# mLSTM by whole chunks of eight heads: queries scaled beforehand, one sum per head, weights of the late query/key units split ahead

## The chip, the cores and the metric

One core of a Trainium2 chip. The metric is the device time of one execution in microseconds. Before the change three executions took 1109.45, 1111.19 and 1111.83 us.

## The reference, cut to what matters

Two decoder layers on 512 tokens of width 1024. Layer 0 mixes tokens with an mLSTM (eight heads, query/key width 64, value width 128), layer 1 with sliding-window attention; each is followed by a gated MLP with a short convolution, and each half has RMSNorm before and behind it. The change lies in the mLSTM. Per head and chunk, with q already times 1/8:

```python
b = jnp.cumsum(lfb, axis=-1)
inter = b + m[..., None]
dlog = b[..., :, None] - b[..., None, :] + igb[..., None, :]
dlog = jnp.where(causal, dlog, -jnp.inf)
m_t = jnp.maximum(inter, jnp.max(dlog, axis=-1))
w = jnp.einsum('bhtd,bhsd->bhts', qb, kb) * jnp.exp(dlog - m_t[..., None])
s_inter = jnp.exp(inter - m_t)
num = jnp.einsum('bhts,bhsv->bhtv', w, vb) + s_inter[..., None] * jnp.einsum('bhtd,bhdv->bhtv', qb, C)
den = jnp.sum(w, axis=-1) + s_inter * jnp.einsum('bhtd,bhd->bht', qb, n)
hout = num / jnp.maximum(jnp.abs(den), jnp.exp(-m_t))[..., None]
C_new = decay[..., None, None] * C + jnp.einsum('bhs,bhsd,bhsv->bhdv', ws, kb, vb)
```

The output is then normalised per head, multiplied by sigmoid(o), where o is another projection of the input, and projected by `m_w_out`.

## The kernel before, in words

**Splitting.** Every large product runs as three fast matmuls on operands in two parts: ScalarE rounds a raw weight tile to the high part (`split_hi`, L535), VectorE subtracts it from the raw tile for the low part (`split_lo`, L884), TensorE multiplies hi by hi, hi by lo, lo by hi (L1435 to L1437 in `project`). Weights come as units of 128 x 1024 (512 KB) in a fixed order: four query/key units loaded at once (`first_units`), a gate unit, query/key units 4 to 7, eight value units, eight units of o, eight of `m_w_out`. SP loads a raw unit as soon as the one four places before it in its slot has been split.

**Order.** There is no planner. Each engine has one queue written out by hand in its block (`sync`, `gpsimd`, `scalar`, `vector`, `tensor`), and semaphores join them. An engine works strictly in the order of its block.

**Query/key units.** ScalarE splits units 4 and 5, then takes the row statistics, then the gate chain on 8 x 512 rows (two tanh, an exponential, a logarithm, with table loads), and after that units 6 and 7. VectorE splits 4 and 5, waits for the gate sums, copies units 0 to 3 out of PSUM (`copy_qk`, L965), does the scans of the gates, and then in one loop (L990) splits unit n + 2 and copies unit n.

**mLSTM steps.** Chunks are of 128 tokens (four). The code takes half of the heads at a time: eight steps `s`, chunk `s // 2`, four heads each (`four(s)`). In step `s` TensorE projects unit `s` of o into bank 6 or 7, then in `combine(s)` multiplies queries by the old state C (L1575, banks 3 and 4), keys by values for the new state (L1580), and weights by values for the numerators (L1584, banks 2 and 5); then `keys(s + 1)` (L1560) makes the next scores. VectorE in `outputs` scales the old-state product by exp(inter - m) (L1086), adds the numerators (L1089) and takes the denominators (L1095, L1096), in `state` decays and adds C (L1069, L1070), in `weigh` multiplies scores by exponentials (L1055), in `weights` makes the exponents of the next step (L1046) and in `scale_o` scales unit `s` of o (L1039). ScalarE takes the exponential (L651), splits a weight unit, takes the tanh of o (L667) and the squares of a finished step (`squares`, L628). GpSimd scales o by the head norm (L504) and broadcasts a chunk's rows u to all partitions through DRAM (L490).

**End of the stage.** The last unit of o is projected in two halves of 256 tokens, with the last `combine` and the transposes of chunk 0 (`turn_heads`, L1598) between them. `out_block(c, ...)` (L1629 to L1631) then multiplies chunk c by the eight units of `m_w_out`; in block 0 each unit k is first needed as TensorE comes to it. `scale_heads`, `gate_heads` and `gated_lo` on VectorE and `gated_hi` on ScalarE prepare chunk c.

## Time and profile before

| | |
|---|---|
| median of three runs | 1111.19 us |
| profiled execution | 1110.87 us, its span 1108.6 us |
| TensorE matmul busy | 1095.0 us (99%) |
| VectorE, ScalarE, GpSimd busy | 539.3, 430.7, 45.5 us |
| mean granted TensorE clock | 0.997 |

The span runs from the first to the last instruction; all positions in microseconds count from its start. TensorE is the engine that is almost always busy; the others have idle time of which most costs nothing. What can be gained or lost in a stage is read from what TensorE waits for there and how far apart its matmuls start.

### The profile page before, as it was taken

To read this page: it belongs to the slowest core of one execution; us is meant where nothing else is said; L and a number is where in the kernel's file an instruction comes from. 1 tells how busy PE (TensorE), PEld (TensorE's weight loads), DVE (VectorE), ACT (ScalarE), POOL (GpSimd) and SP (SyncE) were. 2 spreads that over 40 slices of the span, in tenths; PEclk is the share of its full clock that TensorE was granted. 3 is DMA by queue.
4 is the path that set the end of the run, shared out by engine and by line. 5 is a ranking of instruction groups with operands and counts; after the bars stand their busy time and mean duration, and the time that the engine had idled before them with its cause. 6 is when DMAs were issued, how large, how long until landed. Compare 5 with 4: busy or idle time off the path is not lost.

```text
span 1108.6 us, 14797 instructions
## 1 busy us (share of the span) xinstructions
PE 1095.0 (99%) x5562; PEld 912.9 (82%) x5562; DVE 539.3 (49%) x820; ACT 430.7 (39%) x753; POOL 45.5 (4%) x45
## 2 busy tenths in 40 slices
PE   9999999999999999999999999999999999999997
PEld 7788777898888888888889987789888888888886
DVE  6534678654344444333356486664444444423344
ACT  6511356443323232322255277754232323422242
POOL 1000110000000000000002023200000000000000
PEclk9999999999999999999999999999999999999999
DMA  9332226024333323122362542023323232303231
GB/s 283 121 97 77 82 96 203 3 82 124 95 102 88 112 77 114 38 79 99 105 182 67 147 102 77 1 58 95 105 84 113 77 114 77 112 28 103 96 132 77
DMA packets 141509, 108.72 MB, mean 98 GB/s; under 512 B 22424, under 2 KB 127000, under 8 KB 141472
## 3 DMA queue, kind: packets, MB, share of 16 engines
q1 hardware_dynamic: 140576, 105.83, 32.2%
q0 software_dynamic: 608, 2.11, 0.6%
q8 instruction: 25, 0.41, 0.1%
q10 hardware_dynamic: 288, 0.27, 0.1%
q14 instruction: 12, 0.10, 0.0%
HBM read 106.08 MB, written 2.11 MB: 98 GB/s over the span
## 4 chain that ended last, share of the span: by engine, by line
PE 92%; DVE 4%; ACT 3%; issue 1%; POOL 0%; DVEq 0%; ACTq 0%; POOLq 0%
PE ps L1435 17%; PE ps L1437 17%; PE ps L1436 17%; PE ps L1686 7%; PE ps L1685 7%; PE ps L1684 7%; PE ps L1629 3%; PE ps L1631 2%; PE ps L1630 2%; PE ps L1519 1%; PE ps L1521 1%; PE ps L1520 1%; PE ps L1774 1%; PE ps L1803 1%; PE ps L1785 1%; DVE w_lo L884 1%
## 5 line engine op out<-in xcount | busy, mean ns | idle before, releaser
L1435 PE MATMUL ps<-act_hi,w_hi 128*128 128x512 f32 (+1 forms) x1016 | 369.2, 363 | 2.8 <-DVE w_lo L884 2.6
L1436 PE MATMUL ps<-act_lo,w_hi 128*128 128x512 f32 (+1 forms) x1016 | 367.0, 361 | 0.0
L1437 PE MATMUL ps<-act_hi,w_lo 128*128 128x512 f32 (+1 forms) x1016 | 366.9, 361 | 0.0
L1435 PEld LDWEIGHTS ps<-act_hi,w_hi 128*128 128x128 f32 x1016 | 192.1, 189 | 33.8 <-DVE w_lo L884 3.1
L1437 PEld LDWEIGHTS ps<-act_hi,w_lo 128*128 128x128 f32 x1016 | 192.1, 189 | 29.5
L1436 PEld LDWEIGHTS ps<-act_lo,w_hi 128*128 128x128 f32 x1016 | 192.2, 189 | 29.0
L1684 PE MATMUL ps<-w_hi 128*128 128x512 f32 x288 | 112.0, 389 | 0.0
L1685 PE MATMUL ps<-w_lo,w_hi 128*128 128x512 f32 x288 | 112.0, 389 | 0.0
L1686 PE MATMUL ps<-w_hi,w_lo 128*128 128x512 f32 x288 | 112.0, 389 | 0.0
L717 ACT ACTIVATE arena<-ps,vecs 128x512 f32<-128x512 f32 x44 | 34.3, 779 | 188.6 <-PE ps L1437 188.6
L1216 DVE SCALAR_TENSOR_TENSOR arena<-ps,vecs,arena 128x511 f32<-128x511 f32 x44 | 33.0, 749 | 144.5 <-ACT arena L717 144.4
L711 ACT CAST w_hi<-raw 128x1024 fp32r<-128x1024 f32 x80 | 83.1, 1044 | 39.4 <-PE ps L1437 39.4
L1250 DVE TENSOR_TENSOR w_lo<-raw,w_hi 128x1024 fp32r<-128x1024 f32 x32 | 39.2, 1225 | 119.9 <-ACT w_hi L742 119.9
L1208 DVE TENSOR_TENSOR w_lo<-raw,w_hi 128x1024 fp32r<-128x1024 f32 x80 | 94.0, 1217 | 0.2
L535 ACT CAST w_hi<-raw 128x1024 fp32r<-128x1024 f32 x66 | 68.0, 1046 | 64.5 <-PE ps L1437 26.9
L1225 DVE TENSOR_TENSOR arena<-ps,arena 128x512 f32 (+1 forms) x44 | 30.4, 692 | 117.2 <-PE ps L1437 113.5
L742 ACT CAST w_hi<-raw 128x1024 fp32r<-128x1024 f32 x32 | 33.8, 1055 | 129.1 <-PE ps L1686 129.1
L884 DVE TENSOR_TENSOR w_lo<-raw,w_hi 128x1024 fp32r<-128x1024 f32 x64 | 77.0, 1217 | 7.0 <-ACT w_hi L535 7.0
L1685 PEld LDWEIGHTS ps<-w_lo,w_hi 128*128 128x128 f32 x288 | 54.1, 188 | 11.3
L1684 PEld LDWEIGHTS ps<-w_hi 128*128 128x128 f32 x288 | 54.1, 188 | 11.2
L1686 PEld LDWEIGHTS ps<-w_hi,w_lo 128*128 128x128 f32 x288 | 54.1, 188 | 11.1
L721 ACT ACTIVATE arena<-arena 128x512 f32<-128x512 f32 x44 | 27.8, 632 | 79.6 <-DVE arena L1220 79.6
(209 smaller groups left out, 1226.1 us busy)
## 6 DMA issues: line engine op xcount, KB each, us to landing
raw<-in_f_w_up SPq DMA_DIRECT2D x88, 512.0 KB, 4.6
raw<-in_f_w_down SPq DMA_DIRECT2D x44, 512.0 KB, 3.3
raw<-in_m_w_in SPq DMA_DIRECT2D x23, 512.0 KB, 4.6
raw<-in_m_w_out SPq DMA_DIRECT2D x8, 512.0 KB, 3.5
raw<-in_a_w_in SPq DMA_DIRECT2D x16, 256.0 KB, 4.3
raw<-in_a_w_out SPq DMA_DIRECT2D x16, 256.0 KB, 4.7
h<-in_x SPq DMA_DIRECT2D x4, 512.0 KB, 7.2
h<-in_x_turned SPq DMA_DIRECT2D x3, 512.0 KB, 8.0
```

The source lines that it names most:

```text
L535: nc.scalar.copy(w_hi[:, s], raw[:, s % 4]).then_inc(w_hi_done, 1)
L711: nc.scalar.copy(w_hi[:, 4 + s], raw[:, s]).then_inc(w_hi_done, 1)
L717: nc.scalar.activation(cv[:, t], ps[:, 2 * t], ACT.Identity, scale=taps[l][:, 2, bass.ds(f, 1)], bias=taps[l][:, 3, bass.ds(f, 1)]).then_i ...
L884: nc.vector.tensor_tensor(w_lo[:, s], raw[:, s % 4], w_hi[:, s].bitcast(F32), ALU.subtract).then_inc(w_lo_done, 1)
L1208: nc.vector.tensor_tensor(w_lo[:, 4 + s], raw[:, s], w_hi[:, 4 + s].bitcast(F32), ALU.subtract).then_inc(w_lo_done, 1)
L1250: nc.vector.tensor_tensor(w_lo[:, j], raw[:, j], w_hi[:, j].bitcast(F32), ALU.subtract).then_inc(w_lo_done, 1)
L1435: nc.tensor.matmul(dst, uh[:, k], zh, start=(k == 0), stop=False)
L1436: nc.tensor.matmul(dst, uh[:, k], zl, start=False, stop=False)
L1437: ins = nc.tensor.matmul(dst, ul[:, k], zh, start=False, stop=(k == KT - 1))
L1684: nc.tensor.matmul(dst, hi[:, bs], w_hi[:, s, hs], start=start, stop=False)
L1685: nc.tensor.matmul(dst, hi[:, bs], w_lo[:, s, hs], start=False, stop=False)
L1686: return nc.tensor.matmul(dst, lo[:, bs], w_hi[:, s, hs], start=False, stop=stop)
```

## The change

- **Chunks.** `combine`, `keys`, `weigh`, `state`, `outputs`, `weights` and the exponential take a chunk of eight heads at once: four times instead of eight. TensorE projects two units of o in a row, then runs old state, next scores, new state and numerators of the chunk.
- **One sum.** The old-state product and the numerators go into the same place in PSUM (banks 2 to 5) and are added there. For that the queries of chunks 1 to 3 are multiplied by exp(inter - m) before the product, on GpSimd, after the unscaled ones have made their scores. The factors come to all partitions by three more transfers through DRAM (`s_dram`, `s_all`). The factor 1/8 moves into `copy_qk`. VectorE's L1086 and L1089 become two plain copies a chunk.
- **Units split ahead.** ScalarE and VectorE split query/key units 4 to 7 all together, ahead of the gate chain.
- **Last unit of o in halves.** `scale_o`, tanh and the head-norm scale of the last unit run per half. The squares of the last chunk's first half come behind the cast of output unit 4.
- **Places and queues.** C and the factors lie in `h`, so the rows of x for blocks 1 to 3 are loaded at the end of the stage instead of early; `g_col` is loaded by SP, ahead of x, instead of by ScalarE's queue.

```diff
-        ew = arena[:, E:E + 4 * KB].rearrange("p (b t q) -> p b t q", b=2, t=HG)
+        ew = arena[:, E:E + 8 * KB].rearrange("p (b h q) -> p b h q", b=2, h=MH)
         I = E + 4 * KB
-        itmp = arena[:, I:I + HG * DV1].rearrange("p (t q) -> p t q", t=HG)
-        C = arena[:, I + HG * DV1:I + 2 * HG * DV1].rearrange("p (t q) -> p t q", t=HG)
+        h_flat = h[:].rearrange("p b f -> p (b f)")
+        s_all = h_flat[:, D:D + HG * 3 * P].rearrange("p (t q) -> p t q", t=HG)
+        C = h_flat[:, D + HG * 3 * P:D + HG * 3 * P + HG * DV1].rearrange("p (t q) -> p t q", t=HG)
...
+        PAIRS = [(t, g, 2 * t + g) for t in range(HG) for g in range(2)]
+        def out_at(t, g):
+            return 2 + 2 * (t // 2) + g, slice(t % 2 * DV1, (t % 2 + 1) * DV1)
...
+            nc.sync.dma_start(g_col[:], columns[:, 0:KT]).then_inc(g_col_in, 16)
...
             sp.wait_ge(sum_done, KT - 1)
-            for b in range(NB - 1):
-                nc.sync.dma_start(h[:, b], x[0, b * P:(b + 1) * P]).then_inc(x_in[b], 16)
+            nc.sync.dma_start(h[:, 0], x[0, 0:P]).then_inc(x_in[0], 16)
...
-            sp.wait_ge(e_raw, NS)
+            sp.wait_ge(e_raw, NB)
             gains(norm_mix_post[0], norm_ffn_pre[0])
-            sp.wait_ge(os_done, O_UNITS)
-            nc.sync.dma_start(h[:, NB - 1], x[0, (NB - 1) * P:]).then_inc(x_in[NB - 1], 16)
+            sp.wait_ge(os_done, O_UNITS + 1)
+            for b in range(1, NB):
+                nc.sync.dma_start(h[:, b], x[0, b * P:(b + 1) * P]).then_inc(x_in[b], 16)
...
+            pool.wait_ge(row_act, 2)
+            nc.gpsimd.dma_start(s_dram.ap(), rows[:, 6]).then_inc(s_out, 16)
+            pool.wait_ge(s_out, 16)
+            for g in range(2):
+                nc.gpsimd.dma_start(s_all[g * DK:(g + 1) * DK], s_dram.ap()
+                                    .rearrange("(t g) q -> g t q", g=2)[g][:, P:].partition_broadcast(DK))\
+                    .then_inc(s_in, 16)
+            pool.wait_ge(s_in, 32)
             for n in range(O_UNITS):
                 if n in (2, 4):
-                    pool.wait_ge(e_raw, n)
+                    pool.wait_ge(e_raw, n // 2)
                     u_everywhere(n // 2 + 1)
+                for half in range(2 if n == O_UNITS - 1 else 1):
+                    ts = slice(half * S // 2, (half + 1) * S // 2) if n == O_UNITS - 1 else slice(0, S)
+                    pool.wait_ge(o_tanh, n + half + 1)
+                    nc.gpsimd.tensor_scalar(o_sig[:, n, ts], o_sig[:, n, ts], hn_half[:, n:n + 1],
+                                            hn_half[:, n:n + 1], ALU.mult, ALU.add).then_inc(o_done, 1)
+                if n in (1, 3, 5):
+                    c = n // 2 + 1
+                    pool.wait_ge(st_mm, c + 1)
+                    q_c = qk_t[:, 0:HG, c * P:(c + 1) * P]
+                    nc.gpsimd.tensor_tensor(q_c, q_c, s_all[:, :, (c - 1) * P:c * P], ALU.mult)\
+                        .then_inc(qs_done, 1)
...
-            split_hi(g_qk(4))
-            split_hi(g_qk(5))
+            for n in range(FIRST, QK_UNITS):
+                split_hi(g_qk(n))
...
-            for n in range(6, QK_UNITS):
-                split_hi(g_qk(n))
...
+            exponents(0)
+            for c in range(NB):
+                split_hi(G_O + 2 * c + 1)
+                if c >= 1:
+                    squares(2 * c - 2)
+                tanh_o(2 * c, 2 * c + 1)
+                if c < NB - 1:
+                    exponents(c + 1)
+                    split_hi(G_O + 2 * c + 2)
+                else:
                     for k in range(2):
                         split_hi(G_MOUT + k)
...
+                if c >= 1:
+                    squares(2 * c - 1)
+                if c < NB - 1:
+                    tanh_o(2 * c + 1, 2 * c + 2)
+                if c == NB - 2:
                     nc.scalar.preload_act_table_set(LN_EXP_SET)
                     rms_heads(1, slice(0, 2 * MH))
                     nc.scalar.preload_act_table_set(EXP_TANH_SET)
...
+            tanh_o(NS - 1, NS, 0, S // 2)
+            for k in range(2, 4):
+                split_hi(G_MOUT + k)
+            gated_hi(0, 0)
+            tanh_o(NS - 1, NS + 1, S // 2, S)
             nc.scalar.preload_act_table_set(LN_EXP_SET)
             split_hi(G_MOUT + 4)
             gated_hi(0, 1)
+            squares(NS - 2)
             squares(NS - 1)
             split_hi(G_MOUT + 5)
...
-            split_lo(g_qk(4))
-            split_lo(g_qk(5))
+            for n in range(FIRST, QK_UNITS):
+                split_lo(g_qk(n))
...
-                nc.vector.tensor_tensor(qk_t[:, n], ps[:, qk_bank(n)], rs_row, ALU.mult).then_inc(pj_used, 1)
+                if n < HG:
+                    ins = nc.vector.scalar_tensor_tensor(qk_t[:, n], ps[:, qk_bank(n)], DK ** -0.5, rs_row,
+                                                         ALU.mult, ALU.mult)
+                else:
+                    ins = nc.vector.tensor_tensor(qk_t[:, n], ps[:, qk_bank(n)], rs_row, ALU.mult)
+                ins.then_inc(pj_used, 1)
...
             for n in range(FIRST, QK_UNITS):
-                split_lo(g_qk(n + 2) if n + 2 < QK_UNITS else G_V + n + 2 - QK_UNITS)
                 copy_qk(n)
+                if n >= QK_UNITS - 2:
+                    split_lo(G_V + n - (QK_UNITS - 2))
...
+            def weigh(c):
+                dve.wait_ge(e_exp, c + 1)
+                dve.wait_ge(st_mm, c + 1)
+                e = ew[:, c % 2].rearrange("p (g t) q -> p g (t q)", g=2)
+                nc.vector.tensor_tensor(e, ps[:, 0:2], e, ALU.mult).then_inc(w_done, 1)
+            def state(c):
                 if c == NB - 1:
                     return
+                dve.wait_ge(n_mm, c + 1)
+                new = ps[:, 2:2 + HG, STATE]
                 if c == 0:
+                    ins = nc.vector.tensor_copy(C, new)
                 else:
+                    dec = decay_own[:, :, c].unsqueeze(2).to_broadcast([P, HG, DV1])
+                    link(nc.vector.tensor_tensor(C, C, dec, ALU.mult))
+                    ins = nc.vector.tensor_tensor(C, C, new, ALU.add)
                 ins.then_inc(c_done, 1)
...
+            def outputs(c):
+                dve.wait_ge(n_mm, c + 1)
+                for a in range(2):
+                    ins = nc.vector.tensor_copy(
+                        v_tok[:, c, 4 * a:4 * a + 4].rearrange("p (b g) v -> p g b v", g=2),
+                        ps[:, 2 + 2 * a:4 + 2 * a, 0:2 * DV1].rearrange("p g (b v) -> p g b v", v=DV1))
                 ins.then_inc(num_done, 1)
+                dve.wait_ge(num_done, c + 1)
+                den = v_tok[:, c, :, DV]
                 link(nc.vector.scalar_tensor_tensor(dtmp[:], den, -1.0, den, ALU.mult, ALU.max))
+                link(nc.vector.tensor_tensor(dm[:, c], dtmp[:], gt[:, c, 3], ALU.max))
...
             weights(0)
...
+            for c in range(NB):
+                if c >= 1:
+                    outputs(c - 1)
+                    state(c - 1)
+                weigh(c)
+                split_lo(G_O + 2 * c + 1)
+                if c < NB - 1:
+                    weights(c + 1)
+                else:
+                    finish_factors(1, 0, 2)
+                    scale_heads(0)
+                scale_o(2 * c, (w_used, counted(G_O + 2 * c)))
+                if c < NB - 1:
+                    split_lo(G_O + 2 * c + 2)
+                    scale_o(2 * c + 1, (w_used, counted(G_O + 2 * c + 1)))
+                if c == NB - 2:
                     head_factors(0, 2)
-                if s < NS - 1:
-                    scale_o(s)
-            finish_factors(1, 0, 2)
-            scale_heads(0)
+            split_lo(G_MOUT)
+            scale_o(NS - 1, (oh_mm, 1), 0, S // 2)
+            split_lo(G_MOUT + 1)
             split_lo(G_MOUT + 2)
-            outputs(NS - 1)
+            outputs(NB - 1)
             gate_heads(0, 0)
             scale_heads(1)
             gated_lo(0, 0)
-            scale_o(NS - 1)
+            gate_heads(0, 1)
+            scale_o(NS - 1, (w_used, counted(G_O + NS - 1)), S // 2, S)
             split_lo(G_MOUT + 3)
-            gate_heads(0, 1)
             split_lo(G_MOUT + 4)
             gated_lo(0, 1)
             head_factors(2, NB)
...
+            def keys(c):
+                cs = slice(c * P, (c + 1) * P)
+                if c >= 1:
+                    pe.wait_ge(w_done, c)
+                for t, g, hd in PAIRS:
                     pr = slice(g * DK, (g + 1) * DK)
+                    ins = nc.tensor.matmul(ps[:, g, t * P:(t + 1) * P], qk_t[pr, HG + t, cs], qk_t[pr, t, cs],
+                                           start=True, stop=True)
                 ins.then_inc(st_mm, 1)
+            def combine(c):
                 cs = slice(c * P, (c + 1) * P)
                 if c > 0:
+                    pe.wait_ge(num_done, c)
+                    pe.wait_ge(c_done, c)
+                    pe.wait_ge(qs_done, c)
+                    for t, g, hd in PAIRS:
                         pr = slice(g * DK, (g + 1) * DK)
+                        bank, cols = out_at(t, g)
+                        nc.tensor.matmul(ps[:, bank, cols], qk_t[pr, t, cs], C[pr, t], start=(t % 2 == 0),
+                                         stop=False)
                 if c < NB - 1:
+                    keys(c + 1)
+                    for t, g, hd in PAIRS:
                         pr = slice(g * DK, (g + 1) * DK)
...
+                        nc.tensor.matmul(ps[pr, 2 + t, STATE], kw[:, c, hd * DK:(hd + 1) * DK],
+                                         v_tok[:, c, hd], start=(c == 0), stop=False)
+                pe.wait_ge(w_done, c + 1)
+                for t, g, hd in PAIRS:
+                    bank, cols = out_at(t, g)
+                    ins = nc.tensor.matmul(ps[:, bank, cols], ew[:, c % 2, HG * g + t], v_tok[:, c, hd],
+                                           start=False, stop=(t % 2 == 1))
                 ins.then_inc(n_mm, 1)
...
                 if s < NS - 1:
                     project(SLOT[g], 6 + s % 2).then_inc(w_used, 1)
-                    combine(s)
-                    keys(s + 1)
+                    if s % 2:
+                        combine(s // 2)
                 else:
-                    project(SLOT[g], 6 + s % 2, 0, S // 2)
-                    combine(s)
+                    project(SLOT[g], 6 + s % 2, 0, S // 2).then_inc(oh_mm, 1)
+                    combine(NB - 1)
                     turn_heads(0)
+                    pe.wait_ge(os_done, NS)
                     project(SLOT[g], 6 + s % 2, S // 2, S).then_inc(w_used, 1)
...
```

## Rows read from the trace of the kernel before

**Rows 1.** The page, part 1: busy us (share) and instructions of each engine.

```profile
PE 1095.0 (99%) x5562; PEld 912.9 (82%) x5562; DVE 539.3 (49%) x820; ACT 430.7 (39%) x753; POOL 45.5 (4%) x45
```

**Rows 2.** Windows: length, busy us (instructions) PE, PEld, DVE, ACT, POOL; clock, DMA, GB/s.

```profile
46.70:49.90 3.20, 3.13 (x8) 2.51 (x9) 2.61 (x5) 3.20 (x9) 0.92 (x2) 0.53 0.61 172
...
106.28:188.68 82.40, 80.62 (x506) 64.86 (x505) 62.42 (x123) 40.10 (x106) 7.40 (x10) 1.00 0.39 122
...
175.00:189.00 14.00, 12.84 (x57) 9.85 (x58) 12.33 (x18) 9.45 (x20) 1.01 (x1) 1.00 0.82 243
```

**Rows 3.** TensorE's waits: line, releaser: us in total, times, longest us.

```profile
PE ps L1435 <- DVE w_lo L884: 2.6, 1, 2.6
...
PE ps L1629 <- DVE w_lo L884: 1.1, 2, 0.9
...
PE ps L1598 <- DVE arena L1117: 0.4, 1, 0.4
```

**Rows 4.** Timeline, TensorE, 43 to 50: start, us, instruction, [idle before <- releaser].

```profile
43.75 0.39 PE L1437 MATMUL ps<-act_hi,w_lo 128*128 128x512 f32 x1
46.77 0.79 PE L1435 MATMUL ps<-act_hi,w_hi 128*128 128x512 f32 x1 [2.63 <-DVE w_lo L884]
...
49.85 0.39 PE L1436 MATMUL ps<-act_lo,w_hi 128*128 128x512 f32 x1
```

**Rows 5.** Timeline, VectorE: the low half of unit 6.

```profile
45.51 1.21 DVE L884 TENSOR_TENSOR w_lo<-raw,w_hi 128x1024 fp32r<-128x1024 f32 x1
```

**Rows 6.** Timeline, TensorE, one mLSTM step; the second L1580 row is cut at 129.65.

```profile
128.89 0.72 PE L1575 MATMUL ps<-arena 64*128 64x129 f32 x8
129.54 0.66 PE L1580 MATMUL ps<-arena 128*64 128x129 f32 x8
...
129.70 0.50 PE L1580 MATMUL ps<-arena 128*64 128x129 f32 x6
...
130.13 1.16 PE L1584 MATMUL ps<-arena 128*128 128x129 f32 x8
131.22 0.71 PE L1560 MATMUL ps<-arena 64*128 64x128 f32 x8
131.86 0.50 PE L1435 MATMUL ps<-act_hi,w_hi 128*128 128x512 f32 x1
```

**Rows 7.** Groups of ScalarE, 20 to 240: shapes, count | busy, mean ns | idle before.

```profile
L535 ACT CAST w_hi<-raw 128x1024 fp32r<-128x1024 f32 x32 | 32.6, 1043 | 33.7 <-PE ps L1521 25.0 <-PE ps L1437 7.8 <-DMA raw<-in_m_w_in 0.8
L628 ACT ACTIVATE junk<-arena 128x128 bf16<-128x128 f32 x32 | 9.4, 294 | 0.0
```

**Rows 8.** Timeline, VectorE, behind the numerators of one step.

```profile
148.65 0.70 DVE L1086 TENSOR_TENSOR arena<-ps,gt 128x516 f32<-128x516 f32 x1 [1.64 <-PE ps L1584]
...
150.11 0.17 DVE L1095 SCALAR_TENSOR_TENSOR dtmp<-arena 128x4 f32<-128x4 f32 x1
...
150.51 0.43 DVE L1069 TENSOR_TENSOR arena<-arena,decay_own 128x258 f32<-128x258 f32 x1
...
151.31 0.68 DVE L1055 SCALAR_TENSOR_TENSOR arena<-ps,arena 128x512 f32<-128x512 f32 x1
151.91 1.13 DVE L1046 SCALAR_TENSOR_TENSOR arena<-g_pre,gt,causal 128x128 f32<-128x128 f32 x4
```

**Rows 9.** Groups of VectorE, 20 to 240: one that reads 1024 columns of PSUM.

```profile
L917 DVE TENSOR_TENSOR act_lo<-ps,act_hi 128x1024 fp32r<-128x1024 f32 x4 | 4.9, 1222 | 6.8 <-ACT act_hi L568 6.8
```

**Rows 10.** Groups of GpSimd over the span.

```profile
L504 POOL TENSOR_SCALAR arena<-arena,hn_half 128x512 f32<-128x512 f32 x8 | 6.4, 796 | 120.0 <-ACT arena L667 120.0
...
L516 POOL TENSOR_TENSOR arena<-arena,asm 128x512 f32<-128x512 f32 x4 | 4.2, 1040 | 50.1 <-DVE asm L1357 50.1
```

**Rows 11.** The line of u's broadcasts, L490: from issue to landing.

```profile
DMA to landing us min/median/max: 3.9/5.2/7.6
```

**Rows 12.** Timeline, GpSimd: the last hn scale, beside a split on VectorE.

```profile
176.86 1.01 POOL L504 TENSOR_SCALAR arena<-arena,hn_half 128x512 f32<-128x512 f32 x1 [9.64 <-ACT arena L667]
```

**Rows 13.** Timeline, TensorE: the first matmul of output block 0.

```profile
175.80 0.48 PE L1629 MATMUL ps<-w_hi,act_hi 128*128 128x512 f32 x1
```

More of the change, by code:

```diff
@@ L570, in norm_hi @@
                     .then_inc(z_hi, 1)
-            nc.scalar.dma_start(g_col[:], columns[:, 0:KT]).then_inc(g_col_in, 16)
             nc.scalar.dma_start(raw[:, 0, 0:HALF], m_w_in[0, 0:P, 0:HALF]).then_inc(w_first_in, 16)
@@ L623, in squares @@
                 c = s // 2
-                act.wait_ge(num_done, s + 1)
+                act.wait_ge(num_done, s // 2 + 1)
                 if s >= 1:
                     act.wait_ge(sq_done, s)
-                for n, (_, _, hd) in enumerate(four(s)):
+                for n, hd in enumerate(range(4 * (s % 2), 4 * (s % 2) + 4)):
                     ins = nc.scalar.activation(junk[:, n], v_tok[:, c, hd, 0:DV],
@@ L1034, in _, with scale_o @@
                 copy_v(1, b)
-            def scale_o(s):
-                dve.wait_ge(w_used, counted(G_O + s))
-                nc.vector.tensor_tensor(o_sig[:, s], ps[:, 6 + s % 2], rs_row, ALU.mult).then_inc(os_done, 1)
-            def weights(s):
-                c = s // 2
+            def scale_o(s, ready, lo=0, hi=S):
+                dve.wait_ge(*ready)
+                nc.vector.tensor_tensor(o_sig[:, s, lo:hi], ps[:, 6 + s % 2, lo:hi], rs_row[:, lo:hi],
+                                        ALU.mult).then_inc(os_done, 1)
@@ L1121, in gate_heads @@
                 dve.wait_ge(ht_mm, c + 1)
-                dve.wait_ge(o_done, 4 * half + 4)
+                dve.wait_ge(o_done, 4 * half + 4 + (half if c >= 2 else 0))
                 ks = slice(4 * half, 4 * half + 4)
@@ L1137, in _ @@
             weights(0)
-            for s in range(NS):
-                if s >= 1:
-                    outputs(s - 1)
-                    state(s - 1)
-                weigh(s)
-                if s + 1 < NS:
-                    weights(s + 1)
-                    split_lo(G_O + s + 1)
-                if s == NS - 2:
-                    for k in range(2):
-                        split_lo(G_MOUT + k)
-                if s == NS - 3:
+            for c in range(NB):
[14 more added lines that the diff above has]
+                if c == NB - 2:
                     head_factors(0, 2)
-                if s < NS - 1:
-                    scale_o(s)
-            finish_factors(1, 0, 2)
-            scale_heads(0)
+            split_lo(G_MOUT)
+            scale_o(NS - 1, (oh_mm, 1), 0, S // 2)
+            split_lo(G_MOUT + 1)
             split_lo(G_MOUT + 2)
-            outputs(NS - 1)
+            outputs(NB - 1)
             gate_heads(0, 0)
@@ L1574, in combine @@
                         pr = slice(g * DK, (g + 1) * DK)
-                        nc.tensor.matmul(ps[:, INTER[g], (t % 2) * DV1:(t % 2 + 1) * DV1],
-                                         qk_t[pr, t, cs], C[pr, t], start=True, stop=True)
+                        bank, cols = out_at(t, g)
+                        nc.tensor.matmul(ps[:, bank, cols], qk_t[pr, t, cs], C[pr, t], start=(t % 2 == 0),
+                                         stop=False)
                 if c < NB - 1:
-                    for t, g, hd in four(s):
+                    keys(c + 1)
@@ L1593, in turn_heads @@
                 if c == 1:
-                    pe.wait_ge(num_done, NS)
+                    pe.wait_ge(num_done, NB)
                 if c >= 2:
```

103 lines of the change are left out of this document (18 added, 85 removed).

## The prediction

> **What bounds the kernel now.** I read the page first. TensorE is busy for 1095.0 of 1108.6 us [rows 1], so time can leave this kernel in two ways only: TensorE waits less (or runs less of its time at the lower clock), or it has less to issue. 
>
> The mLSTM stage proper runs from the first score matmuls at 106.28 to the second output block at 188.68 (82.4 us in [rows 2]). TensorE hardly waits there, so VectorE's and ScalarE's savings are worth nothing in it unless they end a wait; what counts is the number of TensorE groups and what becomes late.
>
> **The time of the sum.** All is summed against the profiled execution, 1110.87 us (span 1108.6, 2.3 around it). The median of the runs is 1111.19, 0.3 higher; I add that at the end.
>
> **1. Units 6 and 7 split ahead: -4.3 us.** Their raw tiles were loaded early already. A ScalarE cast of 1.04 [rows 7] and a VectorE split of 1.22 [rows 5] each now stand ahead of the gate chain. Unit 6 can be done by about 25 us; unit 7 has to wait until TensorE has used slot 3 (about 27.9), so cast 29.0, low half 30.2, still ahead of the gate sums that VectorE waits to copy at 31.5. TensorE needs them at 43.8 and 49.2. What is late next there: the low half of the first value unit, now behind the copy of unit 6 (49.3 + 0.7 + 1.2 = 51.2) and needed at 54.7; the second one 56.6 against 60.1. Both are covered, so I take all 4.3. Bounds: 0 if another wait takes its place, 4.3 if none.
>
> **2. g_col on SP's queue, ahead of x: -0.2.** ScalarE's queue issues the first weight tile about 0.44 us earlier, SP's x tiles come that much later; the warm-up matmuls keep TensorE until about 5.5 and the first real one started at 5.8. Between -0.3 and +0.4; I take -0.2. The two x loads fewer at 21 us free DMA time nobody waits for.
>
> **3. Whole chunks: fewer group starts on TensorE, -3.9.** The multiplications are the same in number: no matmul goes or comes. But TensorE changes group less often. In one step [rows 6] four heads of old state take 128.89 to 129.54 (0.65), four of new state 0.59, four of numerators 1.09, four of scores 0.64. Their pairs of f32 matmuls follow at 0.11: dropping the first pair takes 0.16 off the group (0.66 to 0.50) and the other three pairs take 0.50, of which the last matmul's own length is 0.28: (0.50 - 0.28) / 2 = 0.11 a step. So four more pairs add only 0.42 to 0.44 to scores and states (I take 0.42), and eight more matmuls 8 x 0.112 = 0.90 to numerators (1.16 - 0.28 = 0.88 for seven steps, the first of about 0.21). A group start saved is 0.22 (scores, old state), 0.17 (new state), 0.19 (numerators); two projections in a row save another 0.22 (0.09 ahead of the group, 0.11 to 0.13 behind it). Groups saved: scores 4, old state 3, new state 3, numerators 4, project-to-project 4: 0.88 + 0.66 + 0.51 + 0.76 + 0.88 = 3.7. The first scores now take 1.07 and cover the 0.2 wait for the last value copy. Sum -3.9. The sum in one bank instead of two costs TensorE nothing that a row shows; bounds for the whole term -4.5 to -1.
>
> **4. VectorE inside a chunk: +0.2.** Per chunk the first thing due is the low half of unit 2c+1, at one projection, 5.58 us, after the numerators' end. Ahead of it stand now, from [rows 8] by start-to-start steps: wake 0.10, two copies 0.60 + 0.73, the two denominator operations 0.40, state 0.73 + 0.60 at 516 columns (258 columns take 0.43, 516 take 0.70; the step behind a chained one is 0.73, behind an unchained one of 512 it is 0.60), weigh over 1024 columns 1.14 (nearest row: L917, 1.22 long [rows 9]), split 1.22 with its signal 0.05. That is 5.57 against 5.58 for chunks 2 and 3; chunk 1 has no multiply and is 0.7 early. I take 0.1 each. Behind it `weights` for eight heads takes 2.1 and the next units are ready 3.8 us early, so nothing else in the chunk is on the path.
>
> **5. GpSimd's prescale and its transfers: 0.** The three multiplies of 128x512 cost about 1.04 each, as GpSimd's others of that size [rows 10], the two broadcasts are issued near 55 us and used after 120. The chain for chunk c is tanh, hn scale 0.8, prescale 1.04 and a signal, then u's broadcast for chunk 2 (issue 0.6, landing 3.9 to 7.6 us later, 5.2 in the middle [rows 11]). It is behind two instructions more than before; VectorE will wait for it about 1 us before `weights(2)`, within the 3.8 us of slack. Prescaled queries are ready some 5 us or more ahead of their products. Bounds 0 to +3.
> GpSimd and VectorE do get in each other's way in this trace: the hn scale that met a split took 1.01 [rows 12] where the mean of all eight is 0.80 [rows 10]. The Trainium skill, page SBUF — State Buffer, section Who interferes with whom, says that a VectorE instruction with two SBUF inputs and a GpSimd one that reads SBUF exclude each other for their whole length; the trace agrees by that row. It speaks against moving work to GpSimd: by it each prescale that meets a split delays VectorE by up to 1.0, and if two fell in the first 5.6 us of a chunk the sum would be 2 us higher. By my order of times they fall where VectorE waits for TensorE, so the sum doesn't use it.
>
> **6. The end of the stage: +3.0.** Here VectorE and ScalarE set the pace already: TensorE waits 0.4 for `scale_heads(1)` and 1.1 for low halves of the output weights [rows 3]; PE's idle time there is 14.00 less 12.84 us [rows 2]. Call E the start of projection 6. VectorE: low half of unit 7 at E+5.6, factors and `scale_heads(0)` to 6.8, `scale_o(6)` to 7.5, then it waits for ScalarE: tanh 8.1, first output cast 9.1. Split to 10.35, `scale_o` half 10.7, second split 11.85, third (cast 12.5) 13.7, outputs of the whole last chunk 1.33 + 0.4 to 15.45, gate 16.05, `scale_heads(1)` done 17.3. TensorE: 5.58 + 2.9 (half of unit 7) + 1.07 + 1.99 + 0.8 (transposes) + 3.0 = E+15.4. So it waits 1.9 where it waited 0.4: +1.4.
> Then block 0 of the output starts at 18.1 and wants weight k=5 at 25.0. ScalarE: tanh of the last half 19.3 (it waits for `scale_o` at 18.85), table 20.6, k=4 cast 21.6, gated 22.2, now both squares (2 x 1.17: four ACTIVATEs and four accumulator reads each, 0.29 a step [rows 7]) 24.5, k=5 cast 25.5. VectorE: k=4 22.9, head factors 25.15, k=5 26.8, factors and `scale_heads(2)` 28.05, k=6 29.2, k=7 30.35, two gates, cast, low half: 32.4. TensorE waits 1.8, 0.9 and 0.3, and block 1 starts at 32.5, 14.4 after block 0. Before, it was 188.68 - 175.80 = 12.9 [rows 13] with pure matmul work of about 11.0. So +1.5, rounded with the first to 3.0. This is the least certain term; bounds: +0.5 (chains overlap better than I have them) to +6 (each of the waits also halves the clock, at the 1.5 that it cost at 47 us; waits of 0.4 and 0.9 here left it at 1.00 [rows 2], one of 2.6 did not, and 1.9 lies between). A clock drop after the first wait would mostly be swallowed by the second, which ends by VectorE anyway, so I add none.
>
> Afterwards the kernel is as before. The x rows of blocks 1 to 3 are now issued near E+21 and are wanted from E+45 on: covered.
>
> **Sum.** -4.3 - 0.2 - 3.9 + 0.2 + 0 + 3.0 = -5.2: 1105.7 in the profiled frame, 1106.0 against the median.
>
> **Rivals.**
> A. *The end of the stage eats the merge.* Waits there cost 6 instead of 3. For: VectorE's long serial list after the last half unit, and both squares now ahead of the k=5 cast. Against: the second wait hides part of the first. 1110.87 - 5.2 + 3 + 0.3 = 1109.0. Chance 0.15.
> B. *The end costs next to nothing* (0.5), since a slower ScalarE step than mine isn't there. For: my list takes each wait at its worst. 1103.5. Chance 0.12.
> C. *The stop at 44 us only moves*, to unit 7 or the first value unit. For: unit 7's slot comes free at 27.9 only. Against: 13 to 20 us of slack. 4 lost: 1110. Chance 0.05.
> D. *Slower: VectorE's chunk chain.* It stands 0.01 us from the limit. If a prescale meets a split (0.2 extra in the one meeting that the rows show, up to its own 1.04 if the two exclude each other) or a 516- or 1024-wide operation over four banks takes longer than the narrow rows say, each of chunks 1 to 3 gives TensorE a wait, and from waits somewhere above 0.9 the clock falls for 1.5 more. It decides from 1.0 us of lateness with clock drops (3 x 2.5 = 7.5 > 5.2), from 1.8 without. With 1.5 late and drops 3 x 3.0 = 9: 1115.0. Against: the widths are plain multiples of measured ones. Chance 0.08.
> Forecast: 0.60, own range 1104.3 to 1107.8.
>
> **How the numbers follow.** A measurement of this kernel can tell about 0.2% (2.2 us) from no change. Faster than 1109.0: forecast 0.60, B 0.12, half of A 0.08, giving 0.80. Within 0.2%: the other half of A, C, giving 0.12. Slower: D, 0.08. The range 1102.8 to 1109.3 takes in B and A and leaves out C and D and some of the tails.
>
> **What would show it.** Right: no wait for L884 between 44 and 47 us and no stretch at the lower clock there; numerators, scores and states as groups of 16 at 1.99, 1.07, 1.07, 1.02; start of the scores to start of block 1 shorter by 0.7 (82.4 to 81.7). Wrong: waits of over 0.5 us behind each even projection (step 4, D); a first value unit that TensorE waits for (C); PSUM groups that last twice as long (step 3); waits of other sizes than 1.9, 1.8, 0.9 in the output block (step 6).

## The result, and the profile after

The changed kernel takes 1103.9 us (median of 4 runs, 1103.78 to 1104.34) where the kernel before took 1111.16 in the same comparison (4 runs, 1109.45 to 1111.83): ratio 0.9938, 95% interval 0.9921 to 0.9955. Forecast were 1106.0 and a range of 1102.8 to 1109.3. The profiled execution took 1103.78 (span 1102.0) against 1110.87 (1108.6): 7.1 less where the sum said 5.2.

The page's part 1, to be held against [rows 1], says that TensorE has 5.8 us less of busy time at the same number of instructions:

```profile
PE 1089.2 (99%) x5562; PEld 911.0 (83%) x5562; DVE 532.7 (48%) x797; ACT 430.8 (39%) x750; POOL 51.5 (5%) x52
```

The windows that answer to [rows 2] (length, TensorE's busy us and matmuls, granted clock, DMA share, GB/s). The first is the place of the old stop, the second reaches from the first score matmul to output block 1, the third is output block 0:

```profile
46.70:49.90 3.20, 3.20 (x16) 1.00 0.07 13
101.95:182.91 80.96, 76.54 (x506) 1.00 0.41 131
168.54:182.91 14.37, 11.76 (x52) 1.00 0.84 273
```

The stop is gone: 16 matmuls where there were 8, at clock 1.00 instead of 0.53. The stage, from the first score matmul to output block 1, lasts 80.96 instead of 82.40; TensorE is busy for 4.08 less in it and idle for 2.64 more (4.42 against 1.78). The list of TensorE's waits, answering to [rows 3], names what is idle time now (line, releaser, us in total, times, longest). L1656 is the output block, L1624 the transposes of the heads, L1140 `scale_heads`, L916 `split_lo`:

```profile
PE ps L1656 <- DVE w_lo L916: 2.6, 2, 1.7
...
PE ps L1624 <- DVE arena L1140: 1.7, 1, 1.7
```

TensorE's timeline of one chunk, which answers to [rows 6] (start, us, line, tile). L1600 is the old state, L1586 the scores, L1606 the new state, L1611 the numerators:

```profile
129.18 1.16 PE L1600 MATMUL ps<-h,arena 64*128 64x129 f32 x16
130.18 1.06 PE L1586 MATMUL ps<-arena 64*128 64x128 f32 x16
131.16 1.10 PE L1606 MATMUL ps<-arena 128*64 128x129 f32 x16
132.20 2.05 PE L1611 MATMUL ps<-arena 128*128 128x129 f32 x16
134.00 0.48 PE L1461 MATMUL ps<-act_hi,w_hi 128*128 128x512 f32 x1
```

From start to start the groups take 1.00, 0.98, 1.04 and 1.80. The prediction had 1.07, 1.07, 1.02 and 1.99. The end of the stage on TensorE, with the three waits in brackets:

```profile
162.09 1.04 PE L1624 MATMUL ps<-ident,arena 128*128 128x128 f32 x8
...
167.69 1.09 PE L1624 MATMUL ps<-ident,arena 128*128 128x128 f32 x8 [1.71 <-DVE arena L1140]
168.54 0.48 PE L1656 MATMUL ps<-w_hi,act_hi 128*128 128x512 f32 x1
...
177.40 0.47 PE L1656 MATMUL ps<-w_hi,act_hi 128*128 128x512 f32 x1 [1.74 <-DVE w_lo L916]
...
179.88 0.47 PE L1656 MATMUL ps<-w_hi,act_hi 128*128 128x512 f32 x1 [0.86 <-DVE w_lo L916]
...
182.91 0.50 PE L1656 MATMUL ps<-w_hi,act_hi 128*128 128x512 f32 x1
```

What ScalarE (the squares, then the cast of weight 5) and VectorE (the low half of weight 5, then `scale_heads(2)`, with the low half of weight 6 behind it at 178.52) do ahead of the second and third wait:

```profile
172.41 0.31 ACT L646 ACTIVATE junk<-arena 128x128 bf16<-128x128 f32 x1
...
174.97 1.03 ACT L556 CAST w_hi<-raw 128x1024 fp32r<-128x1024 f32 x1
...
176.03 1.22 DVE L916 TENSOR_TENSOR w_lo<-raw,w_hi 128x1024 fp32r<-128x1024 f32 x1 [0.26 <-ACT w_hi L556]
...
177.38 1.23 DVE L1140 TENSOR_TENSOR arena<-arena,fac 128x1024 f32<-128x1024 f32 x1
```

VectorE in a chunk, which answers to [rows 8]: two copies of the products, the denominators (not shown), the state, the weighing, and the low half that TensorE needs at 139.6. From the first copy to the end of the low half it is 138.50 + 1.21 - 134.29 = 5.42, with the wake of 0.10 5.52, where the prediction added up 5.57:

```profile
134.29 1.30 DVE L1112 COPY arena<-ps 128x516 f32<-128x516 f32 x2 [4.09 <-PE ps L1611]
...
136.03 0.69 DVE L1104 TENSOR_TENSOR h<-h,decay_own 128x516 f32<-128x516 f32 x1
136.76 0.69 DVE L1105 TENSOR_TENSOR h<-h,ps 128x516 f32<-128x516 f32 x1
137.37 1.22 DVE L1092 TENSOR_TENSOR arena<-ps,arena 128x1024 f32<-128x1024 f32 x1
138.50 1.21 DVE L916 TENSOR_TENSOR w_lo<-raw,w_hi 128x1024 fp32r<-128x1024 f32 x1
```

GpSimd's prescale, answering to [rows 10]: 1.28 each instead of 1.04, and no engine waits for it:

```profile
L525 POOL TENSOR_TENSOR arena<-arena,h 128x512 f32<-128x512 f32 x3 | 3.8, 1276 | 0.0
```

**Where the 7.1 us went.** The scores start at 101.95 instead of 106.28: -4.33. From there to block 1: -1.44. From block 1 to the last matmul nothing changes (5.77 ahead at either end). Behind the last matmul the span is 0.83 shorter, and what lies outside the span 0.5 shorter (1.8 against 2.3).

How early TensorE gets through its first work differs from execution to execution, so positions of different profiles are best compared from a common point. A group of eight small matmuls stands at 32 us, ahead of the old stop; in the kernel before and in the changed one:

```profile
32.16 0.95 PE L1489 MATMUL ps<-ones,arena 128*128 128x1 f32 x8
32.14 0.95 PE L1515 MATMUL ps<-ones,arena 128*128 128x1 f32 x8
```

In the eight profiles of the experiments it starts between 32.30 and 33.10. From it to the first scores it is 74.12 us in the kernel before and 69.81 in the changed one: the stop is worth 4.31.

### The profile page after: what moved, and what is told of

It is laid out like the page before. It is cut to its first block, busy times and chain, and to the rows that moved or that the text cites. A ratio compares the mean times of both kernels' runs of the same rounds, so it can differ in the third digit from the quotient of the medians.

```text
span 1102.0 us, 14768 instructions
## 1 busy us (share of the span) xinstructions
PE 1089.2 (99%) x5562; PEld 911.0 (83%) x5562; DVE 532.7 (48%) x797; ACT 430.8 (39%) x750; POOL 51.5 (5%) x52
## 4 chain that ended last, share of the span: by engine, by line
PE 92%; DVE 4%; ACT 3%; issue 0%; POOL 0%; DVEq 0%; ACTq 0%; POOLq 0%
PE ps L1461 17%; PE ps L1462 17%; PE ps L1463 17%; PE ps L1713 7%; PE ps L1711 7%; PE ps L1712 7%; PE ps L1656 3%; PE ps L1657 2%; PE ps L1658 2%; PE ps L1545 1%; PE ps L1547 1%; PE ps L1546 1%; PE ps L1801 1%; PE ps L1830 1%; PE ps L1812 1%; ACT w_hi L556 1%
## 5 line engine op out<-in xcount | busy, mean ns | idle before, releaser
L916 DVE TENSOR_TENSOR w_lo<-raw,w_hi 128x1024 fp32r<-128x1024 f32 x64 | 77.3, 1219 | 20.4 <-ACT w_hi L556 20.3
```

The source lines that it names most:

```text
L916: nc.vector.tensor_tensor(w_lo[:, s], raw[:, s % 4], w_hi[:, s].bitcast(F32), ALU.subtract).then_inc(w_lo_done, 1)
```

## Experiments

All are timed beside the kernel before, the first four on one chip (before: 1110.75), the others on a second (1110.65). The changed kernel's 1103.9 is from its own comparison (before: 1111.16). The medians of the kernel before lie 0.5 apart, so what differs by less than that between variants is read from the traces and not from the times.

**e1_stop_back** puts the splits of units 6 and 7 behind the gate chain again, all else as changed.

```diff
-            for n in range(FIRST, QK_UNITS):
-                split_hi(g_qk(n))          # ScalarE; the same in VectorE's list
+            split_hi(g_qk(4))
+            split_hi(g_qk(5))
...
-                copy_qk(n)
-                if n >= QK_UNITS - 2:
-                    split_lo(G_V + n - (QK_UNITS - 2))
+                split_lo(g_qk(n + 2) if n + 2 < QK_UNITS else G_V + n + 2 - QK_UNITS)
+                copy_qk(n)
```

> The changed kernel (1103.9) with query/key units 6 and 7 split behind the gate chain again. Theory: the stop of TensorE near 44 us comes back whole, 2.6 to 3.0 us of wait and a stretch at the lower clock: 1103.9 + 4.3 = 1108.2. Rival (the stop is covered by the rest of the change, its gain is elsewhere): under 1 us, 1104 to 1105.

**e2_only_ahead** is the kernel before with that edit alone, the other way round.

> The kernel before (1111.2) with query/key units 4 to 7 split ahead of the gate chain and nothing else. Theory: 1111.2 - 4.3 = 1106.9, the wait for the low half at 44 us gone, everything behind it as before. Rival (split ahead only pays with the x loads moved away or with whole chunks): 0 to -2, 1109 to 1111.

Measured: e1 1109.05 (11 runs, 1106.7 to 1109.29; ratio to before 0.9981, 0.9972 to 0.999), 5.15 above the changed kernel. e2 1106.4 (5 runs; ratio 0.9963, 0.9949 to 0.9977), 4.35 below the kernel before. e1's waits at the end of the stage, its stop, and the clock behind the stop:

```profile
PE ps L1657 <- DVE w_lo L918: 2.6, 2, 1.8
...
PE ps L1625 <- DVE arena L1141: 1.7, 1, 1.7
```

```profile
47.60 0.50 PE L1462 MATMUL ps<-act_hi,w_hi 128*128 128x512 f32 x1 [2.63 <-DVE w_lo L918]
```

```profile
49.00:52.40 3.40, 3.40 (x10) 0.54 0.87 270
```

The stop is back with its 2.63 us and a stretch at the lower level, and the end of the stage doesn't notice: its waits are the same 2.6 and 1.7. So the two parts of the change are independent. From the group at 32 us to the first scores it is 69.81 in e2, as in the changed kernel, and 74.36 in e1: the stop costs 4.55 there. The 5.15 of the medians is more, and the profiles say where some of it can come from: e1's group at 32 us starts 0.85 later than the changed kernel's, and the lateness is there before 10 us, ahead of anything that the edit touches (e2's starts 0.94 later than that of the kernel before in the same way).

The cost of the stop isn't one number. 2 of the 11 runs of e1 took 1106.70 and 1106.75 at a mean clock of 0.999 and 1.0, the others about 1109.1 at 0.998; of the 15 runs of before beside them two took 1108.54 and 1108.81 at 0.999, the others about 1110.9 at 0.997. This fits one and the same wait of 2.6 us being followed by the lower clock in most executions, not in all, with a difference of about 2.3. It is a reading of times: no run of the lower kind was profiled, and in the profiles the slow stretch itself costs 1.5 (before) and 1.8 (e1: 4.55 less the 2.79 of the wait).

**e3_four_heads** keeps everything of the change but has TensorE do a chunk's products in two rounds of four heads (old state, scores, new state, numerators, twice).

```diff
+                for own in (PAIRS[:4], PAIRS[4:]):
+                    ...old state, keys(c + 1, own), new state, numerators for t, g, hd in own
```

> The changed kernel with TensorE's work of a chunk in two rounds of four heads (old state, next scores, new state, numerators, twice), all other engines untouched, projections still two in a row. Theory (what whole chunks save is group starts on TensorE): by the group lengths 4 heads 0.65, 0.54, 0.59, 1.09 against 8 heads 1.00, 0.99, 1.03, 1.81, so about +0.9 us for chunks 1 and 2, somewhat less for 0 and 3: +2.5 to +3.3, 1106.4 to 1107.2. Rival (the saving lies in VectorE's fewer instructions or in the single sum): no change, 1103.9.

Measured: 1106.01 (5 runs, 1105.29 to 1106.19; ratio 0.9958, 0.9945 to 0.9972), 2.1 above the changed kernel. Its timeline of one chunk's first round, the start and the end of the second:

```profile
130.54 0.72 PE L1603 MATMUL ps<-h,arena 64*128 64x129 f32 x8
131.09 0.61 PE L1586 MATMUL ps<-arena 64*128 64x128 f32 x8
131.63 0.66 PE L1609 MATMUL ps<-arena 128*64 128x129 f32 x8
132.22 1.16 PE L1614 MATMUL ps<-arena 128*128 128x129 f32 x8
133.31 0.71 PE L1603 MATMUL ps<-h,arena 64*128 64x129 f32 x8
...
135.00 1.16 PE L1614 MATMUL ps<-arena 128*128 128x129 f32 x8
135.91 0.48 PE L1461 MATMUL ps<-act_hi,w_hi 128*128 128x512 f32 x1
```

The two rounds last 135.91 - 130.54 = 5.37, the merged groups 4.82. Merging itself saves 0.55 a chunk (0.39 in the last), 2.0 in all and less than the 0.9 a chunk expected; 0.4 of it the wait for `scale_heads(1)` gives back (1.3 instead of 1.7 here), so the stage is 1.6 longer in this trace. The 2.1 of the medians holds other differences too: this execution reaches the group at 32 us 0.8 later than the changed kernel's.

The rest of step 3 is not from merging a chunk's groups. Part of it is the order in which groups stand. Old state takes 0.55 here where it took 0.65 [rows 6]: the scores that follow it have the same stationary shape (the tile that is held in the array, 64\*128, the first pair in a row). And numerators take 0.91 with a projection behind them, 0.99 with the transposes behind them, 1.09 with scores or old state.

**e6_scores_behind_state** tests just that: the changed kernel with the next chunk's scores behind the new state.

```diff
                 if c < NB - 1:
-                    keys(c + 1)
                     for t, g, hd in PAIRS:
                         ...new state...
+                    keys(c + 1)
```

> The changed kernel with the score matmuls of the next chunk behind the new state's, not directly behind the old state's. Theory (a group pays a start of about 0.1 us when the shape of the stationary tile changes, and none when the group before has the same one): the 16 score matmuls of chunks 2 and 3, which took 0.99 behind the old state, take 1.09, as those of chunks 0 and 1; the new state stays at 1.03; the total grows by 0.1 to 0.2, which only the trace can tell. Rival (the length hangs on the PSUM banks or on the place in the chunk): 0.99 stays, or the numerators grow instead. The time 1103.5 to 1104.6 by both.

Measured: 1104.45 (4 runs, 1104.30 to 1104.58; ratio 0.9946, 0.9931 to 0.9962), 0.55 above.

```profile
129.43 1.16 PE L1600 MATMUL ps<-h,arena 64*128 64x129 f32 x16
130.53 1.10 PE L1605 MATMUL ps<-arena 128*64 128x129 f32 x16
131.56 1.16 PE L1586 MATMUL ps<-arena 64*128 64x128 f32 x16
132.65 2.05 PE L1611 MATMUL ps<-arena 128*128 128x129 f32 x16
```

Old state 1.10 and scores 1.09 instead of 1.00 and 0.98: a start of 0.1 ahead of each of the two, so 0.2 a chunk, 0.41 from the first scores to projection 6 (48.74 against 48.33). The times agree (0.55). The theory expected this of the scores alone and so had half the size; the rival (banks, place) falls. That it is the shape, and not the 64 rows that both groups use, is not separated here: the one other order, new state (128\*64) beside either, pays the start.

**e5_prescale_twice** adds GpSimd work ahead of each prescale.

```diff
+                    extra = h_flat[:, 3076:3572].rearrange("p (t q) -> p t q", t=HG)
+                    s_c = s_all[:, :, (c - 1) * P:c * P - 4]
+                    nc.gpsimd.tensor_tensor(extra, s_c, s_c, ALU.mult)
```

> The changed kernel with one more GpSimd multiply of 128x496 (prescale factors times themselves, into unused columns) ahead of each of the three prescales. GpSimd takes 1.27 us for each prescale in the changed kernel, so three times about 1.2 us more, and the broadcast of u for the next chunk is issued 1.2 us later. Theory (step 5, GpSimd is covered): VectorE may wait up to 1 us for u at the weights of chunks 2 and 3, inside 3.8 us of slack, and the time stays at 1103.9, between 1103.4 and 1104.4. Rival (GpSimd holds VectorE up, or the transfer is on the path): each of the two or three chunks pays about 1 us, 1106 to 1107.5, with TensorE waiting behind the even projections.

Measured: 1103.79 (4 runs, 1103.46 to 1103.94; ratio 0.994, 0.9925 to 0.9955). TensorE's waits are those of the changed kernel. GpSimd, then VectorE's wait for the transfer of u:

```profile
117.45 1.01 POOL L527 TENSOR_TENSOR h<-h 128x496 f32<-128x496 f32 x1
118.43 1.28 POOL L528 TENSOR_TENSOR arena<-arena,h 128x512 f32<-128x512 f32 x1
119.67 0.60 POOL L495 DMA_DIRECT2D g_post<-u_dram  x1
```

```profile
DVE arena L1086 <- DMA g_post<-u_dram: 0.9, 1, 0.9
```

The added 1.0 us makes VectorE wait 0.9 for u once, and nothing comes of it: TensorE doesn't wait for what stands behind. So step 5's cover holds and is at least 0.9 deep beyond what the change uses. In the changed kernel itself VectorE doesn't wait for u at all.

**e8_split_first** and **e9_heads_first** each take one move out of the reordered kernel below. e8 is this; e9 moves `scale_heads(1)` ahead of `split_lo(G_MOUT)` and `split_lo(G_MOUT + 2)` behind `gate_heads(0, 0)`.

```diff
-                weigh(c)
                 split_lo(G_O + 2 * c + 1)
+                weigh(c)
```

> The changed kernel with VectorE's low half of the odd gate unit ahead of the weighing of the scores, in every chunk (one part of the reordered kernel). Theory: this takes away the waits of 0.2 us ahead of the odd projections of chunks 1 to 3 (step 4) and leaves the end of the stage as it is: 0.6 less, 1103.3. TensorE's waits of 1.7, 1.7 and 0.9 at the end stay. Rival (the chain of VectorE inside the chunk is what makes the end late, too): 2 or more less, 1102 or below, and the waits at the end shrink.

> The changed kernel with only two moves in VectorE's list at the end of the stage: the scaling of heads of chunk 1 ahead of the first two output weights' low halves, and the third low half behind the gating of heads. Theory (step 6: the first wait of 1.71 us is VectorE's order, the second of 1.74 and third of 0.86 are ScalarE's order: squares ahead of the cast of weight 5): the first wait goes, VectorE's copies come 0.7 to 2 earlier, the second and third stay at 2.6 together; 1.7 less, 1102.2. Rival (ScalarE's chain alone sets the end; what the first wait gives is given back at weight 5): second and third wait grow to 4.3 together and the time stays at 1103.9.

Measured, e8: 1103.65 (5 runs, 1103.07 to 1104.37; ratio 0.994, 0.9926 to 0.9953), 0.25 less where the theory said 0.6, and too little for the times to tell; in the trace the stage is 0.35 shorter (80.61). Its waits at the end, and TensorE's clock just behind the first:

```profile
167.49 1.09 PE L1624 MATMUL ps<-ident,arena 128*128 128x128 f32 x8 [2.03 <-DVE arena L1140]
...
177.21 0.47 PE L1656 MATMUL ps<-w_hi,act_hi 128*128 128x512 f32 x1 [0.22 <-DVE w_lo L916]
179.69 0.47 PE L1656 MATMUL ps<-w_hi,act_hi 128*128 128x512 f32 x1 [0.87 <-DVE w_lo L916]
```

```profile
168.94:172.29 3.35, 3.35 (x9) 0.51 0.34 97
```

The waits of chunks 2 and 3 went (projection pair 11.45 to 11.09, the next one and a half 8.82 to 8.51: 0.67 together), but the 0.3 of the last chunk came back at once as a longer wait for `scale_heads(1)`. And this execution shows what the prediction argued of a clock drop here: behind 2.03 us of waiting the clock fell to 0.51, the matmuls of that stretch followed each other at 0.43 instead of 0.23 (1.6 us in all), and the wait for weight 5 fell from 1.74 to 0.22. From projection 6 to block 1 it is 32.66 against 32.63. That drop cost nothing.

Measured, e9: 1102.65 (5 runs, 1102.36 to 1104.90; ratio 0.9934, 0.992 to 0.9947). Three runs lie at 1102.36 to 1102.65, two at 1104.8 and 1104.9; the profile is of the last kind:

```profile
176.14 0.47 PE L1656 MATMUL ps<-w_hi,act_hi 128*128 128x512 f32 x1 [1.85 <-DVE w_lo L916]
178.62 0.77 PE L1656 MATMUL ps<-w_hi,act_hi 128*128 128x512 f32 x1 [0.85 <-DVE w_lo L916]
```

```profile
179.18:184.30 5.12, 5.12 (x14) 0.50 1.18 300
```

No wait for `scale_heads(1)`; the other two are 2.7 together as before, not 4.3. So the first wait was the order in VectorE's list and the other two are another matter: the theory holds, with 1.3 to 1.5 gained in three runs against 1.7 expected (in the trace block 0 starts 1.92 earlier, counted from the first scores). In the profiled execution the clock fell behind the last two waits, where no later wait swallows it: the matmuls there follow at 0.43, and from weight 6 to the next transposes it is 9.63 instead of 7.24, 2.4 us more. I can't show that the other high run has the same cause, and the mean clock doesn't tell: it is 0.997 in both high runs and in two of the three low ones.

**e4_end_reordered** is the version that beats both kernels: the moves of e8 and e9, ScalarE's list at the end with the casts ahead of what only later blocks need, and VectorE's low half of weight 6 ahead of `scale_heads(2)`.

```diff
 ScalarE, behind tanh_o(NS - 1, NS, 0, S // 2) and split_hi 2, 3:
-            gated_hi(0, 0), tanh_o(second half), table load, split_hi(4), gated_hi(0, 1),
-            squares(NS - 2), squares(NS - 1), split_hi(5), rms_heads(2), split_hi 6, 7
+            gated_hi(0, 0), split_hi(4), squares(NS - 2), gated_hi(0, 1), tanh_o(second half),
+            squares(NS - 1), split_hi 5, 6, table load, rms_heads(2), split_hi(7)
 VectorE:
-            split_lo(G_MOUT + 5), finish_factors(2, 2, NB), scale_heads(2), split_lo 6, 7
+            split_lo 5, 6, finish_factors(2, 2, NB), scale_heads(2), split_lo(7)
```

> The changed kernel with another order at the end of the stage: scale_heads(1) straight behind scale_o(6), the last outputs ahead of the split of output unit 2, output unit 4 cast ahead of the last tanh, units 5 and 6 ahead of the second table load and of scale_heads(2), the first squares of the last chunk before the last tanh; and split_lo(2c+1) ahead of weigh in each chunk. Theory (waits of 1.7, 1.7 and 0.9 there are due to the order of VectorE and ScalarE, not to their load): most of the waits go, -3.5 to -5: 1099 to 1100.5. Rival (VectorE and ScalarE are at their limit there): the waits move, within 1 us of 1103.9.

Measured: 1098.57 (4 runs, 1098.02 to 1099.09; ratio to before 0.9893, 0.9878 to 0.9909), 5.3 below the changed kernel by the medians, 4.9 by way of the kernel before. The only wait left there, and block 0's start:

```profile
166.30 0.50 PE L1656 MATMUL ps<-w_hi,act_hi 128*128 128x512 f32 x1
...
177.69 0.50 PE L1656 MATMUL ps<-w_hi,act_hi 128*128 128x512 f32 x1 [0.17 <-DVE act_lo L1156]
```

Block 0 takes 11.39 instead of 14.37. From the first scores to block 1 it is 75.45 instead of 80.96: of these 5.5 about 0.7 are the waits in the chunks, 1.9 the wait for `scale_heads(1)`, and 3.0 block 0 with its waits for weights 5 and 6, which were still there in e9 and went only with the moves in ScalarE's list and of weight 6 in VectorE's. These moves were not tried one by one.

## Why the prediction was right, step by step

**Step 1 (-4.3): right.** From the group at 32 us to the first scores -4.31 in the traces, -4.35 in the times of e2 alone; e1 has 4.55 in its trace and 5.15 in its times. Nothing became late behind it; rival C is out. The size isn't fixed: 2.8 is the wait alone, and the clock behind it adds 1.5 to 1.8 in the two profiles that have it. The forecast took a profiled execution of that kind.

**Step 2 (-0.2): not shown.** The group at 32 us starts at 32.16 before and 32.14 after, but at 33.10 in e2, whose queues are those of before, and between 32.30 and 32.99 in the variants of the changed kernel. A term of 0.2 can't be read against a scatter of 0.9, and no run tried it by itself.

**Step 3 (-3.9): right in kind, too small; this is the term that missed most, -4.9.** The groups' lengths against the forecast's: numerators 1.81 three times and 1.89 for 1.99 each (-0.64), old state 1.00, 1.00, 1.10 for 1.07 (-0.11), scores 1.09, 1.09, 0.99, 0.99 for 1.07 (-0.12), new state 1.03 for 1.02 (+0.04): -0.8. Projections two in a row saved 1.1 instead of 0.9. The prediction priced each group's start as fixed. It hangs on the neighbour: scores beside the old state (same stationary shape) pay no start, and numerators with a projection behind them take 0.18 less than with scores or old state behind them (0.91 for the second eight of e3, 1.09 for the first). Taken apart by the traces of before, e3 and after, merging a chunk's groups is worth 2.0, the order in which groups stand 1.3 (old state 0.4, scores 0.4, numerators 0.5), projections in a row 1.1, and the first scores of all heads at once 0.5, of which 0.2 is the wait that they cover.

**Step 4 (+0.2): right in kind, 0.67.** The sum of VectorE's steps was within 0.05 of the trace, and it stood at the limit as said; what a chain at its limit costs was undersized (e8: 0.36 and 0.31). Rival D would have needed 1.0 a chunk; no prescale met a split in the chunks (116 to 150 in the trace); the clock stayed at 1.00.

**Step 5 (0): right** (e5), though the prescale takes 1.28, not 1.04, and the wait of about 1 us for u that it allowed VectorE didn't come. Of the last unit's two half hn scales the first met only the last 0.20 us of a split on VectorE and took 0.62. The second met one for 0.58 (the split ran from 169.09 to 170.30) and took 1.01; in e4 it met the last 0.1 us of a split, a whole second one and another subtraction in a row (up to 170.05) and took 2.17 (the third line is e4's):

```profile
162.07 0.62 POOL L519 TENSOR_SCALAR arena<-arena,hn_half 128x256 f32<-128x256 f32 x1 [2.59 <-ACT arena L674]
...
169.72 1.01 POOL L519 TENSOR_SCALAR arena<-arena,hn_half 128x256 f32<-128x256 f32 x1 [7.03 <-ACT arena L674]
168.22 2.17 POOL L519 TENSOR_SCALAR arena<-arena,hn_half 128x256 f32<-128x256 f32 x1 [5.62 <-ACT arena L674]
```

It ended 0.43 behind the split here and 0.34 behind the last subtraction in e4. That is the rule of the Trainium skill, page SBUF — State Buffer, section Who interferes with whom, that the prediction weighed, and on GpSimd's side the traces agree. The split itself took its usual 1.21, so that VectorE is held up no row shows; in these two meetings it had started first.

**Step 6 (+3.0): right, +2.8** (1.3 ahead of block 0, where the half projection and its wait take 4.81 instead of 3.54, and 14.37 instead of 12.88 in block 0). Waits of 1.9, 1.8 and 0.9 were forecast, and 1.71, 1.74 and 0.86 came; the last of 0.3, ahead of block 1, didn't (its first matmul follows at 0.41, as before the change). The first is VectorE's order (e9). The second ends with the low half of weight 5, whose cast stands at 174.97 directly behind 2.6 us of squares; the third with that of weight 6, behind VectorE's `scale_heads(2)` at 177.38. Both went in e4, which moved these and other things at once. Rival A wanted 6 and B 0.5.

**Sum.** In the stage -4.9 + 0.7 + 2.8 = -1.4 for the forecast -0.7. So of the 1.9 us by which the profiled execution beats the sum 0.7 is step 3 less steps 4 and 6, and 1.3 lies behind the last matmul and outside the span, less 0.2 of steps 1 and 2. The eight profiles of the experiments tell those two apart. From the last matmul's start to the end e2, which is the kernel before but for one edit, has 6.24 us, all others 5.7 to 6.1, the changed kernel 6.1; only the one profiled execution of the kernel before has 6.95: that points to scatter of that execution. Outside the span every run of the experiments has 2.0 to 2.4 with the kernel before and e2, and 1.7 to 1.9 with the seven made from the changed kernel, as with that kernel itself: that 0.5 came with the change, and with which part of it stays open.

So the time came out where it did partly by luck: 1103.9 lies in the stated range, but below the forecast's own 1104.3 to 1107.8 and beside rival B's 1103.5. B's reason is refuted all the same, since the end of the stage cost 2.8 and not 0.5. What made up the difference is 1.0 more from step 3, and 1.3 for which the prediction had no term.

## What to carry to other kernels

Price a TensorE group by its neighbours: standing groups with one stationary shape side by side and putting the numerators ahead of a projection gave 1.3 us here, beside the 2.0 of merging. When work in a stage is merged, the engines behind it get their input later and in one lump; look at what the last lump's consumers have queued ahead of it, for here a reorder of two lists gave about 5 us, some two thirds as much as the whole change. And a wait of 2 to 3 us costs its length and, in some executions, 1.5 to 2.4 us of lower clock behind it; that second part was free only where a later wait for another engine swallowed it (e8).

## What was not expected of the hardware

Old state and scores, 64\*128 tiles both, take 0.2 us less side by side than apart (e6). A wait of 2.63 us was followed by the lower clock in both profiles that have it, and in 13 of 15 runs of the kernel before if their times are read so; shorter ones did so in single executions: 2.03 us (e8), 1.85 and 0.85 six matmuls apart (e9), while 1.74 to 1.76 with the same 0.85 behind it did not in the profiles of the changed kernel, e1, e3, e5 and e6. GpSimd's multiply took 1.28 us on 128x512 in four separate pieces of columns per row and 1.01 on a 128x496 whose output is contiguous (e5). A GpSimd instruction of 0.62 us took 2.17 beside a row of VectorE subtractions that read SBUF twice (e4).
